# Meta tokens turned in the tenth slot, the root's spread between the halves of the first keys' quarter, scores of both row blocks together, and other orders in the attention tails of a two-block transformer kernel

## The reference

```python
for i in range(DEPTH):                       # DEPTH = 2
    hn = rmsnorm(h, norm_mix[i])
    mix = diff_attention(hn, ...) if i % 2 == 0 else neighborhood_attention(hn, ...)
    h = h + mix
    h = h + swiglu(rmsnorm(h, norm_ffn[i]), ffn_w_gate[i], ffn_w_up[i], ffn_w_down[i])
    gate = jax.nn.sigmoid(rmsnorm(h, norm_ple[i]) @ ple_w_gate[i])
    h = h + gate * (p[i] @ ple_w_proj[i])
# second block: 16 meta tokens are put ahead of the 256
h = jnp.concatenate([meta, x], axis=1)
xn = rms_norm(h, norm_mix_g[layer])          # also for the meta tokens
# ... forgetting attention and a convolution on xn, output product, feed-forward
```

## Time and profile before

| | |
|---|---|
| runs, median (lowest to highest) | 1014.9 us (1014.52 to 1014.96), 3 runs |
| the profiled execution, its own time | 1015.26 us |
| its span in the profile | 1013.4 us |
| mean granted clock of TensorE | 0.997 of full |
| PE busy | 993.4 us, 98% of the span |
| DVE busy, ACT busy | 635.6 us (63%), 506.4 us (50%) |
| POOL busy | 129.3 us (13%) |
| transfers | 174.77 MB, mean 172 GB/s |

### The profile page before, as it was taken

The page is one execution under the profiler, slowest core; times in us unless marked ns, Lnnn a source line. Parts: engine busy times, 40 slices in busy tenths (PEclk is TensorE's granted clock), DMA queues, the critical chain, the costliest instruction groups (busy, mean ns, idle before and its releaser), DMA issues.

```text
span 1013.4 us, 14604 instructions
## 1 busy us (share of the span) xinstructions
PE 993.4 (98%) x5869; PEld 865.7 (85%) x5869; DVE 635.6 (63%) x981; ACT 506.4 (50%) x751; POOL 129.3 (13%) x207
## 2 busy tenths in 40 slices
PE   7999999999999999999999999999999999999997
PEld 6889788888888898988888888888989889999995
DVE  6867677555556875555765555568665877555554
ACT  7666745444444655554544444456564355434442
POOL 5000796800000000000000000012500000000000
PEclk9999999999999999999999999999999999999999
DMA  9944469955555564243475555545643337656521
GB/s 277 299 136 143 104 154 209 301 175 199 179 195 177 176 204 145 111 126 125 150 244 178 195 181 193 183 132 195 191 163 110 100 125 253 204 168 205 171 81 42
DMA packets 112724, 174.77 MB, mean 172 GB/s; under 512 B 5977, under 2 KB 73569, under 8 KB 112657
## 3 DMA queue, kind: packets, MB, share of 16 engines
q1 hardware_dynamic: 106224, 165.43, 51.0%
q0 software_dynamic: 6272, 8.15, 3.3%
q10 hardware_dynamic: 160, 0.27, 0.1%
HBM read 172.77 MB, written 1.05 MB: 172 GB/s over the span
## 4 chain that ended last, share of the span: by engine, by line
PE 91%; DVE 5%; ACT 2%; DMA 1%; issue 1%; SPq 0%; DVEq 0%; ACTq 0%
PE bank L1017 27%; PE bank L1019 27%; PE bank L1018 27%; PE bank L1130 2%; DVE wl L1531 1%; PE bank L1160 1%; PE bank L1032 1%; PE bank L1187 1%; DMA raw<-in_da_w_qkv_dram 1%; PE bank L1246 1%; PE bank L1193 1%; PE bank L1180 1%; PE bank L1140 1%; ACT wh L607 1%; PE bank L1163 0%
## 5 line engine op out<-in xcount | busy, mean ns | idle before, releaser
L1531 DVE TENSOR_TENSOR wl<-raw,wh 128x2048 fp32r<-128x2048 f32 x154 | 355.2, 2312 | 185.2 <-ACT wh L607 185.1
L607 ACT ACTIVATE wh<-raw 128x2048 fp32r<-128x2048 f32 x154 | 292.0, 1909 | 118.4 <-PE bank L1019 111.8
L1017 PE MATMUL bank<-wh,xh 128*128 128x512 f32 (+2 forms) x664 | 250.5, 377 | 1.6 <-DVE xl L1608 1.0
L1019 PE MATMUL bank<-wh,xl 128*128 128x512 f32 (+2 forms) x664 | 245.9, 370 | 0.0
L1018 PE MATMUL bank<-wl,xh 128*128 128x512 f32 (+2 forms) x664 | 245.8, 370 | 0.0
L1017 PE MATMUL bank<-xh,wh 128*128 128x256 f32 (+1 forms) x672 | 194.7, 290 | 1.0 <-DVE wl L1847 0.5
L1018 PE MATMUL bank<-xl,wh 128*128 128x256 f32 (+1 forms) x672 | 190.4, 283 | 0.0
L1019 PE MATMUL bank<-xh,wl 128*128 128x256 f32 (+1 forms) x672 | 190.4, 283 | 0.0
L1017 PEld LDWEIGHTS bank<-wh,xh 128*128 128x128 f32 (+1 forms) x664 | 125.2, 189 | 22.6 <-issue 2.0
L1019 PEld LDWEIGHTS bank<-wh,xl 128*128 128x128 f32 (+1 forms) x664 | 125.0, 188 | 22.2
L1018 PEld LDWEIGHTS bank<-wl,xh 128*128 128x128 f32 (+1 forms) x664 | 125.3, 189 | 20.3
(11 more groups left out here) (248 smaller groups left out, 854.4 us busy)
## 6 DMA issues: line engine op xcount, KB each, us to landing
raw<-in_w_ff_dram SPq DMA_DIRECT2D x32, 1024.0 KB, 5.2
raw<-in_ffn_w_gate_dram SPq DMA_DIRECT2D x44, 512.0 KB, 4.0
raw<-in_ffn_w_up_dram SPq DMA_DIRECT2D x44, 512.0 KB, 5.0
raw<-in_ffn_w_down_dram SPq DMA_DIRECT2D x22, 1024.0 KB, 5.0
raw<-in_na_w_qkv_dram SPq DMA_DIRECT2D x12, 1024.0 KB, 5.2
raw<-in_w_in_dram SPq DMA_DIRECT2D x12, 1024.0 KB, 5.2
raw<-in_da_w_qkv_dram SPq DMA_DIRECT2D x11, 1024.0 KB, 11.5
raw<-in_ple_w_gate_dram SPq DMA_DIRECT2D x8, 1024.0 KB, 5.0
```

The lines of the kernel that those rows point to most:

```text
L607: nc.scalar.activation(wh[:, i % RING, :], raw[:, i % RAW, :], ACT.Copy).then_inc(s_hi, 1)
L1017: nc.tensor.matmul(dst, lh, rh, start=start, stop=False, skip_group_check=True)
L1019: return nc.tensor.matmul(dst, ll, rh, start=False, stop=stop, skip_group_check=True)
L1531: nc.vector.tensor_tensor(wl[:, i % RING, :], raw[:, i % RAW, :], wh[:, i % RING, :].bitcast(F32), ALU.subtract).then_inc(s_lo, 1)
```

## The change

- The meta tokens are no longer turned behind the first keys' quarter. DVE norms them in slot 9, behind that slot's (empty) list of steps, and PE turns them into bank 6 behind slot 9. ACT and DVE bring them out in slot 9, DVE behind `k_out`. PE needs the result from slot 10 on, before it was from slot 2 on. The buffers of the tokens, of their gain and of the distances are others.
- `spread_root` of layer 0 is between the two halves of the first keys' quarter.
- In layers 0 and 1, `attention_step` computes the scores of an even step and of the odd step behind it together, the odd one in columns 256 to 511. The even score waits for the shift of the odd step before; the odd one waits for nothing. The even step's shift waits for both scores.
- In `tail_0`, ACT splits the unit ahead of the copy of step 14 (before: behind it and the squares). DVE mixes step 13 ahead of the shift of step 14, and turns the first block ahead of the shift of step 15.
- In `tail_1`, ACT turns each block ahead of the exponentials. DVE turns the first block behind the shift of step 14, then shifts step 15, and only then copies the third group of values out.

```diff
@@ buffers
-        dist_i = b_reg[:, 8 * NEAR:9 * NEAR].bitcast(I32)      # dist_f, dist_n behind it
-        meta_gain = v_reg[0:META, 0:D]
+        dist_i = v_reg[:, 0:NEAR].bitcast(I32)                 # dist_f, dist_n behind it
+        meta_gain = b_reg[0:META, 8 * NEAR + D:8 * NEAR + 2 * D]
-        meta_s = k_reg[0:META, 0:D]
-        meta_n = k_reg[0:META, D:2 * D]
+        meta_s = b_reg[0:META, 8 * NEAR:8 * NEAR + D]
+        META_SLOT = 9
@@ ACT, tail_0
                 exponentials(0, 15)
+                split_to(first["wo", 0] + 4)
                 copy_turned(0, 14)
                 value_squares(2)
-                split_to(first["wo", 0] + 4)
                 copy_turned(0, 15)
@@ ACT, tail_1
                 copy_turned(1, 12)
+                turn_hi("att1", 0, 0)
                 exponentials(1, 14)
-                turn_hi("att1", 0, 0)
                 copy_turned(1, 13)
+                turn_hi("att1", 1, 0)
                 exponentials(1, 15)
-                turn_hi("att1", 1, 0)
@@ ACT, slots (removed ahead of them)
                     for s in steps:
                         attention_step(l, s)
+                    if l == 0 and slot == META_SLOT:
+                        wait(act, turned, "meta", 0, 0)
+                        nc.scalar.activation(xh[:, :, X0 - META:X0], bank[6][:, 0:P]...).then_inc(turned_hi.sem, 1)
@@ PE, score
-                        if s >= 1:
+                        if s >= 2 and b == 0:
                             wait(pe, shifted, l, s - 1)
...
-                            ins = nc.tensor.matmul(bank[4 + m][:, 0:256], q_t[half, g, b * P:(b + 1) * P],
+                            ins = nc.tensor.matmul(bank[4 + m][:, S * b:S * b + S], q_t[half, g, b * P:(b + 1) * P],
@@ PE, attention_step
-                score(l, s)
+                if s % 2 == 0:
+                    score(l, s)
+                    score(l, s + 1)
                 apply(l, s)
@@ PE, first stage
+                keys = quarter("k", 0)
+                if l == 0:
+                    next(keys)
                 spread_root(mix, bank[4])
-                run(quarter("k", 0))
-                if l == 0:
-                    meta_turn()
+                run(keys)
@@ PE, slots
                     if slot == 2:
                         wait(pe, emb_lo, l)
-                        if l == 0:
-                            need("meta", 0, 0)
+                    if l == 0 and slot == META_SLOT + 1:
+                        need("meta", 0, 0)
                     for s in STEPS[slot]:
                         attention_step(l, s)
+                    if l == 0 and slot == META_SLOT:
+                        wait(pe, p_copied, 0, 5)
+                        meta_turn()
@@ DVE, shift
-                    wait(dve, scored, l, s)
+                    wait(dve, scored, l, s + 1 if l < 2 and b == 0 else s)
@@ DVE, tail_0
+                mix(13)
                 shift(0, 14)
-                mix(13)
+                turn_lo("att0", 0, 0)
                 shift(0, 15)
-                turn_lo("att0", 0, 0)
                 mix(14)
@@ DVE, tail_1
                 shift(1, 14)
+                turn_lo("att1", 0, 0)
+                shift(1, 15)
                 values_out(1, 2)
-                shift(1, 15)
-                turn_lo("att1", 0, 0)
                 turn_lo("att1", 1, 0)
@@ DVE, first stage
                     q_over_rms(0)
-                    meta_norm()
-                    wait(dve, normed, "meta", 0, 0)
                     k_out(0)
@@ DVE, slots (the low half is removed ahead of them)
                     for s in steps:
                         attention_step(l, s)
+                    if l == 0 and slot == META_SLOT:
+                        meta_norm()
...
                     split_to(first[part, l, c] + 4)
                     if slot % 2 == 1:
                         {"q": q_over_rms, "k": k_out, "v": v_out}[part](c)
+                    if l == 0 and slot == META_SLOT:
+                        wait(dve, turned_hi, "meta", 0, 0)
+                        nc.vector.tensor_tensor(xl[:, :, X0 - META:X0], bank[6][:, 0:P]..., ALU.subtract)
```

More of the change, by code:

```diff
@@ L196, in two_blocks_kernel @@
         sub_col = sb("sub_col", [P, 1])
-        dist_i = b_reg[:, 8 * NEAR:9 * NEAR].bitcast(I32)
-        dist_f = b_reg[:, 9 * NEAR:10 * NEAR]
-        dist_n = b_reg[:, 10 * NEAR:11 * NEAR]
-        meta_gain = v_reg[0:META, 0:D]
+        dist_i = v_reg[:, 0:NEAR].bitcast(I32)
+        dist_f = v_reg[:, NEAR:2 * NEAR]
+        dist_n = v_reg[:, 2 * NEAR:3 * NEAR]
+        meta_gain = b_reg[0:META, 8 * NEAR + D:8 * NEAR + 2 * D]
         grid_mask = sb("grid_mask", [P, GRID])
@@ L676, in _ @@
             act.wait_ge(s_meta, 32)
-            nc.scalar.activation(meta_n, meta_s, ACT.Square, scale=D ** -0.5,
+            nc.scalar.activation(k_reg[0:META, 0:D], meta_s, ACT.Square, scale=D ** -0.5,
                                  accum_out=stat[0:META, 40:41]).then_inc(sumsq.sem, 1)
@@ L865, in _ @@
                 nc.scalar.activation(ah[:, 512:1024], bank[6][:, :], ACT.Copy).then_inc(emb_hi.sem, 1)
-                if l == 0:
-                    wait(act, turned, "meta", 0, 0)
-                    nc.scalar.activation(xh[:, :, X0 - META:X0], bank[7][:, 0:P].rearrange("p (k s) -> p k s", k=KD),
-                                         ACT.Copy).then_inc(turned_hi.sem, 1)
                 for slot, steps in enumerate(STEPS):
@@ L874, in _ @@
                         attention_step(l, s)
+                    if l == 0 and slot == META_SLOT:
+                        wait(act, turned, "meta", 0, 0)
+                        nc.scalar.activation(xh[:, :, X0 - META:X0], bank[6][:, 0:P].rearrange("p (k s) -> p k s", k=KD),
+                                             ACT.Copy).then_inc(turned_hi.sem, 1)
                     if slot % 2 == 1 and part == "q":
@@ L1298, in meta_turn @@
                 for k in range(KD):
-                    ins = nc.tensor.transpose(bank[7][:, META * k:META * k + META], meta_n[:, k * P:(k + 1) * P],
+                    ins = nc.tensor.transpose(bank[6][:, META * k:META * k + META], meta_s[:, k * P:(k + 1) * P],
                                               ident[0:META, 0:META])
@@ L1673, in shift @@
                             ins = nc.vector.tensor_tensor_reduce(
-                                out=prob[:, s % 3, 256 * m:256 * m + 256], in0=bank[4 + m][:, 0:256],
+                                out=prob[:, s % 3, 256 * m:256 * m + 256], in0=bank[4 + m][:, S * b:S * b + S],
                                 in1=near[:, hd, P - P * b:P - P * b + 256], scale=-1.0, scalar=3.0e38,
@@ L1887, in meta_norm @@
                 inv_root(rstd[0:META, 20:21], stat[0:META, 40:41])
-                nc.vector.scalar_tensor_tensor(out=meta_n, in0=meta_s, scalar=rstd[0:META, 20:21], in1=meta_gain,
+                nc.vector.scalar_tensor_tensor(out=meta_s, in0=meta_s, scalar=rstd[0:META, 20:21], in1=meta_gain,
                                                op0=ALU.mult, op1=ALU.mult).then_inc(normed.sem, 1)
@@ L1952, in _ @@
                                         ALU.subtract).then_inc(emb_lo.sem, 1)
[L1953 to L1956, removed]
                 if l == 0:
@@ L1974, in _ @@
                         {"q": q_over_rms, "k": k_out, "v": v_out}[part](c)
+                    if l == 0 and slot == META_SLOT:
+                        wait(dve, turned_hi, "meta", 0, 0)
+                        nc.vector.tensor_tensor(xl[:, :, X0 - META:X0], bank[6][:, 0:P].rearrange("p (k s) -> p k s", k=KD),
+                                                xh[:, :, X0 - META:X0].bitcast(F32), ALU.subtract).then_inc(turned_lo.sem, 1)
                 if l == 0:
```

## The result

The changed kernel takes **1020.87 us** (median of 4 runs, 1020.59 to 1022.52). The kernel before, run beside it, takes 1014.93 (1014.52 to 1015.57). The ratio is 1.0061, with a 95% interval of 1.0045 to 1.0077: slower by 5.9 us, or 0.6%. The forecast was 1019.9, with a range of 1016.6 to 1022.2. The profiled execution of after took 1021.02, of which 1019.2 are its span.

The account below looks back on a forecast made before the run. TensorE, busy for 98% of the span, was taken as the bound. Terms +3.1 + 1.5 - 1.25 + 1.7 = +5.05 us on the median of 1014.9 gave 1019.9 us, range 1016.6 to 1022.2.

Parts of the forecast that it names:

- Meta tokens in slot 9: Layer 0, slot 9: PE stalls 3.7 us at the meta transposes until DVE's norm is done; net +3.1 us.
- the norm is no wait: Rival: DVE's slot 8 and 9 work ends before PE's slot 9; -0.1, 1014.8, no change; chance 0.12.
- DVE runs ahead: Rival: DVE's queue is 3.7 us ahead by slot 8's end, so PE skips both waits; -2.3, 1012.6; chance 0.08.
- The lead: Layer 0's first stage: of 6.3 us gained by PE, 1.24 is left at step 1's transposes, ready at 49.95.
- No edit moves that transfer: Layer 0's first shift: the unit landing at 37.19 was taken as fixed, so step 3's probabilities come at 49.95 regardless.
- Joint scores at zero: Paired scores in layers 0 and 1: taken as zero, bounds -0.5 (16 pairs, 0.03 each) and +0.5 us.
- The clock: Slow TensorE clock behind the slot 9 stall: one fall counted, +1.5 us, bounds 0 and 3.0.
- the further fall in layer 1's tail: Rival: the clock falls once more, near 47.8 or in layer 1's tail; +6.5, 1021.4; chance 0.13.
- A third: First stage of layer 0: a clock fall at 42.8 would be hidden by the next wait; no size given.
- Layer 0's tail: End of layer 0: ACT's earlier split removes the last product's wait; -1.25 us, bounds 0 and -2.2.
- Layer 1's tail: End of layer 1: step 12's product waits 2.2 us for DVE's later copy-out; +1.7 us, no clock fall counted.

Follow-up runs that it names:

- e7: e4 with DVE splitting each unit one pair of slots later in layer 0's slots 0 to 8; 1006.24 us, ratio 0.9915 to the kernel before.
- e1: The kernel before with the joint scores alone; 1011.29 us, ratio 0.9963 to the kernel before.
- e5: The changed kernel with unread identity transposes on PE, 34 ahead of the meta turn and 18 ahead of layer 1's step 12 product; 1015.54 us.
- e6: The changed kernel with layer 0's tail in the old orders on ACT and DVE; 1020.92 us, ratio 1.0070 to the kernel before.
- e3: The changed kernel with layer 1's tail in the old orders on ACT and DVE; 1016.59 us, ratio 1.0016 to the kernel before.
- e2: The changed kernel with the meta norm back in its old place on DVE, the turn still behind slot 9; 1013.0 us, ratio 0.9981.
- e4: The changed kernel with both the early meta norm and layer 1's old tail orders; 1010.39 us, ratio 0.9951 to the kernel before.
- e8: e4 with the root's spread ahead of the whole first keys' quarter, as before the change; 1011.36 us, ratio 0.9961 to the kernel before.

## Why the prediction was right, point by point

- **Meta tokens in slot 9: right.** The stall was counted from slot 7's scores at 3.7; it is 3.99. The rivals in which the norm is no wait or DVE runs ahead are refuted: DVE's split in front of the norm waited 1.66 for ACT.
- **The lead: right in kind, too large.** 1.24 was predicted, 0.57 came. I took the second mixing as the end of the chain. It ends at 50.12 (49.64 + 0.48), but PE's transposes also wait for ACT's copy of the step before, which starts at 50.11 behind exponentials that waited for the shift:
```profile
49.11 0.51 ACT L701 ACTIVATE prob<-prob,row_neg 128x256 f32<-128x256 f32 x1 [2.06 <-DVE row_neg L1679]
50.11 0.36 ACT L718 ACTIVATE pt<-bank 128x256 f32<-128x256 f32 x1
```
- **"No edit moves that transfer": true of the transfer, wrong as a bound.** e7 shows that the shift need not wait for it at all. It waited because DVE's split of that unit stood in front of it. For the change as made the step holds.
- **Joint scores at zero: the term most mis-sized.** I allowed 0.03 for a pair and looked for a cost in waits. No row stood behind the 0.03. The runs give 0.34 a pair in layer 1 and 3.8 in all (e1), outside the bounds of -0.5 and +0.5. A cost in waits was there too, but in the two tails and smaller. The hint was in the trace of before: 27 of the 32 scores of layers 0 and 1 start 0.20 or 0.21 behind a matmul of a quarter (63.31 to 63.52), where matmuls of one form follow 0.12 apart.
- **The clock: the other mis-sized term.** One fall at 1.5 was counted, as in the earlier trace rows; there were two that PE could not hide, and e5 prices them together at 5.3 (5.8 by the landmarks). Each lasted longer than the one before the change. So what happened is the case of a rival, the further fall in layer 1's tail (chance 0.13, 1021.4), and 1020.87 lies outside the forecast's own narrower range of 1019.2 to 1020.7. That rival had the right mechanism and about half of the size. A third, with a window of 43 to 46 us at 0.57, lies ahead of the next wait and costs little, as the prediction said.
- **Layer 0's tail: right.** -1.25 predicted, -1.20 by the landmarks. e6 gives the order 1.6, of which the pair takes 0.44 back.
- **Layer 1's tail: the wait right, its price not.** A wait of 2.2 was predicted and 2.17 came. Without its fall the tail is 1.5 longer than before (e5), close to the 1.7; with it, 4.6 (after), of which the old orders take 4.3 back (e3).

So 1019.9 was close to 1020.87 partly because two errors cancel: some 3.8 too much for the scores, and some 3.8 too little for the clock (5.3 less 1.5). The sign and the places of the waits are shown by e2, e3 and e5; the nearness of the sum is luck.

## What to carry to other kernels

Price a new wait on TensorE with the slow stretch behind it, not by its length alone; where the wait can't be removed, idle transposes into a free bank kept the clock here (e5). Where a stall is removed on the bounding engine, find which instruction it will stand at next, and ask which work in front of that one's producer could move behind it: here one constant in the split's lead was worth 4.2 us (e7 against e4), where taking away both stalls of the first stage left slot 10's scores at the same 74.02 (e4 and e1). When two edits share a queue, try them apart: this change held 4.7 us of gain (e4 against the kernel before), and two orders, of the norm and of layer 1's tail, that cost 10.5 (after against e4).

## What the runs showed of the hardware that was not expected

- **Falls of the clock** followed waits of PE of 3.82, 2.70, 2.17 and, in e1's profiled execution, of only 0.61 (this window is of e1, behind 449.91):
```profile
451.00:454.00 3.00, 2.80 (x7) 2.28 (x8) 0.74 (x2) 1.05 (x4) 0.00 (x0) 0.54 0.02 5
```
  The same wait of 0.61 in e3, e4 and e8 had none. The wait of 2.55 near 50 us was followed by a fall in e8 (49 to 52 us: 0.70) and by none in e4 (1.00). The slow stretches lasted from 3.3 us (31.85 to 35.18 before) to some 6 us (457 to 463 after). How long one lasts differs even where the order of work around it is the same (layer 1's tail in after and in e6), so a single profile prices it poorly.
- **Matmuls over 64 rows between matmuls over 128** cost 0.72 for a group of four and 1.15 for a group of eight, so about 0.3 belongs to the group and not to its matmuls. In the timeline, the first of a group starts 0.21 behind the matmul in front (62.65 to 62.86), where matmuls of one form follow 0.12 apart. Which part of the engine this belongs to stays open.
